# The second mixer of a two-block transformer on one core: from nineteen blocks between its projections to one block, head by head

## The reference, cut to what matters

```
u_a, v_a, q, k, v = jnp.split(h @ w_in, SPLIT_POINTS, axis=-1)
y_a = gelu(u_a) * (einsum('gtp,bcpgk->bctgk', tril(ws), rms_norm(gelu(v_a))) + bs)
q, k = rms_norm(q, q_norm_g), rms_norm(k, k_norm_g)          # per head of 128
z = einsum('bhqd,bhkd->bhqk', q, k) * 128 ** -0.5
log_fail = where(causal, log_sigmoid(-z), 0)                 # causal: key before query
log_a = log_sigmoid(z) + (sum of log_fail over the keys between key and query)
y_b = einsum('bhqk,bhkd->bhqd', where(causal, exp(log_a), 0), v)
y = rms_norm(concatenate([y_a, y_b]), out_norm_g)            # per group of 128
x = x + gate1 * (y @ w_out)
```

## Time and profile before

| | |
|---|---|
| median of three executions | 2900.5 us |
| the profiled execution, its own time | 2898.79 us |
| its span in the profile | 2897.1 us |
| PE busy, share of the span | 2436.1 us, 84% |
| DVE busy | 1146.4 us, 40% |
| ACT busy | 810.4 us, 28% |
| mean granted TensorE clock | 0.898 |

### The profile page before, as it was taken

The page is one execution under the profiler, slowest core; times in us unless marked ns, Lnnn a source line. Parts: engine busy times, 40 slices in busy tenths (PEclk is TensorE's granted clock), DMA queues, the critical chain, the costliest instruction groups (busy, mean ns, idle before and its releaser), DMA issues. The chain is left out here.

```text
span 2897.1 us, 42631 instructions
## 1 busy us (share of the span) xinstructions
PE 2436.1 (84%) x18072; PEld 1898.3 (66%) x18072; DVE 1146.4 (40%) x1421; ACT 810.4 (28%) x995; POOL 10.7 (0%) x56
## 2 busy tenths in 40 slices
PE   5998778977888978699999999996947577888885
PEld 5995558944875875499999899984833443444442
DVE  3763345533552410254555555554442220111112
ACT  3442323312121320244343443434420110111110
POOL 0000000000000000000000000000000000000000
PEclk8997989988885999899999999997978676999997
DMA  4446642467114322155555545523510469999998
GB/s 177 194 195 269 246 188 117 174 256 317 60 60 174 157 105 116 59 191 187 189 189 189 189 175 203 189 103 140 211 77 0 190 239 415 422 427 427 427 425 350
DMA packets 61371, 610.14 MB, mean 211 GB/s; under 512 B 8850, under 2 KB 9234, under 8 KB 16146
## 3 DMA queue, kind: packets, MB, share of 16 engines
q1 hardware_dynamic: 50114, 572.03, 49.6%
q0 software_dynamic: 1872, 23.07, 2.0%
q10 hardware_dynamic: 9216, 12.60, 1.2%
HBM read 674.76 MB, written 14.68 MB: 238 GB/s over the span
## 5 line engine op out<-in xcount | busy, mean ns | idle before, releaser
L1883 DVE TENSOR_TENSOR ffn_w_lo<-ffn_raw,ffn_w_hi 128x2048 fp32r<-128x2048 f32 x128 | 293.1, 2291 | 234.3 <-ACT ffn_w_hi L1876 234.3
L1876 ACT ACTIVATE ffn_w_hi<-ffn_raw 128x2048 fp32r<-128x2048 f32 x128 | 244.9, 1914 | 360.4 <-PE psum L1915 355.5
L1913 PE MATMUL psum<-u_hi,ffn_w_hi 128*128 128x256 f32 x1024 | 291.0, 284 | 15.1 <-DVE ffn_w_lo L1883 14.0
L1914 PE MATMUL psum<-u_lo,ffn_w_hi 128*128 128x256 f32 x1024 | 290.7, 284 | 0.0
L1915 PE MATMUL psum<-u_hi,ffn_w_lo 128*128 128x256 f32 x1024 | 290.7, 284 | 0.0
L2607 PE MATMUL psum<-moe_raw,moe_x_t 128*32 128x512 f32 x1536 | 216.6, 695 | 80.8 <-DMA moe_raw<-in_moe 73.2
L1913 PEld LDWEIGHTS psum<-u_hi,ffn_w_hi 128*128 128x128 f32 x1024 | 197.6, 193 | 16.0 <-DVE ffn_w_lo L1883 14.2
L1913 PE MATMUL psum<-ffn_w_hi,ffn_hid_hi 128*128 128x512 f32 x512 | 199.4, 389 | 0.0
L1914 PE MATMUL psum<-ffn_w_lo,ffn_hid_hi 128*128 128x512 f32 x512 | 199.4, 389 | 0.0
L1915 PE MATMUL psum<-ffn_w_hi,ffn_hid_lo 128*128 128x512 f32 x512 | 199.2, 389 | 0.0
L1914 PEld LDWEIGHTS psum<-u_lo,ffn_w_hi 128*128 128x128 f32 x1024 | 197.6, 193 | 0.5
(11 more groups left out here) (539 smaller groups left out, 4401.5 us busy)
## 6 DMA issues: line engine op xcount, KB each, us to landing
ring<-in_stream SPq DMA_DIRECT2D x107, 2048.0 KB, 10.9
moe_raw<-in_moe SPq DMA_DIRECT2D x96, 2048.0 KB, 17.0
ffn_raw<-in_ffn SPq DMA_DIRECT2D x128, 1024.0 KB, 4.8
moe_raw<-in_moe POOLq DMA_DIRECT2D x48, 2048.0 KB
expert_rows<-moe_stage ACTq DMA_DIRECT2D x192, 64.0 KB, 8.4
x<-in_x SPq DMA_DIRECT2D x2, 1024.0 KB, 7.8
mem<-in_mem SPq DMA_DIRECT2D x2, 1024.0 KB, 14.7
out<-x SPq DMA_DIRECT2D x2, 1024.0 KB, 4.4
```

Of the source, the lines that this page charges most:

```text
L1876: act.activation(self.w_hi[:, number % self.HIGHS], self.raw[:, number % self.RAWS], ACT.Copy)\
L1883: dve.tensor_tensor(self.w_lo[:, number % self.LOWS], self.raw[:, number % self.RAWS], self.w_hi[:, number % self.HIGHS].bitcast(F32), ALU ...
L1913: pe.matmul(out, lhs[0], rhs[0], start=start, stop=False)
L1914: pe.matmul(out, lhs[0], rhs[1], start=False, stop=False)
```

## The change

The function gets `sem`, to make 26 semaphores. The squares and sums of the groups 1, 2 and 3 are taken within the input projection: DVE does those of group g - 1 between pieces 3 and 4 of group g. Root, reciprocal, scaling and the mask on `ws` follow within that block too, while PE still works on group 4. The squares live in `h_t`, which is free once the input is split. SP no longer waits for the small inputs; DVE does, before the mask.

All that lay between the two projections is one block. q and k norm weights are applied by ACT's copy after the transposes. Per head ACT computes Abs of the scores, Exp of the negative and Ln(1 + e); DVE adds max(z, 0), masks for PE's sums, and subtracts; PE sums over keys in banks 4 to 7; DVE subtracts, ACT takes Exp, DVE masks, PE multiplies with v. The copy of the scores to SBUF and the separate maximum and argument are gone. The gating unit is computed while ACT is at the first heads, and its half of the output norm uses Ln and Exp for the root. The attention half is squared by ACT out of PSUM and scaled by DVE out of PSUM. The output norm's weights are applied as DVE takes the last transposes.

```diff
-def second_mixer(nc, k, io, x, h_t, gate, scope_sb):
+def second_mixer(nc, k, io, x, h_t, gate, scope_sb, sem):
...
+    spare = h_t[:].rearrange("p c t -> p (c t)")
+    squares = spare[:, 0:3 * TT * COLS].rearrange("p (t n) -> p t n", t=TT)
+    proj_summed, proj_root = sem("proj_summed"), sem("proj_root")
...
-            sp.wait_ge(k.small_in, 96)
...
+            def sums(g):
+                own, at = slice((g - 1) * COLS, g * COLS), proj[:, :, g * COLS:(g + 1) * COLS]
+                dve.wait_ge(k.tt_free, 4 + t0 + 2 * g + 2)
+                s.step(dve.tensor_tensor(squares[:, :, own], at, at, ALU.mult))
+                s.settle()
+                dve.tensor_reduce(ssq[:, :, 4 * g - 4:4 * g], squares[:, :, own].rearrange("p t (g n) -> p t g n", n=P),
+                                  AX.X, ALU.add).then_inc(proj_summed, 1)
+
+            def scaled(g):
+                at = proj[:, :, g * COLS:(g + 1) * COLS].rearrange("p t (g n) -> p t g n", n=P)
+                s.step(dve.tensor_tensor(at, at, ssq[:, :, 4 * g - 4:4 * g].unsqueeze(3).broadcast_to([P, TT, 4, P]),
+                                         ALU.mult))
+            s.step(dve.tensor_scalar(qk_norm[:, 0:1], col(k, "q_norm"), P ** -0.5, None, ALU.mult))
+            s.step(dve.tensor_copy(qk_norm[:, 1:2], col(k, "k_norm")))
             for g in range(5):
-                rows.low(dve, g, range(8))
+                rows.low(dve, g, range(4))
+                if g >= 2:
+                    sums(g - 1)
+                rows.low(dve, g, range(4, 8))
+            dve.wait_ge(proj_root, 1)
+            s.step(dve.reciprocal(ssq[:], ssq[:]))
+            s.settle()
+            for g in (2, 3, 1):
+                scaled(g)
+            dve.wait_ge(k.small_in, 96)
+            s.step(dve.tensor_tensor(ws[:], ws[:], const(k, "tri_le").unsqueeze(1).broadcast_to([P, GMLP_GROUPS, P]),
+                                     ALU.mult))
+            s.settle()
 
         @block.scalar
         def _(act):
@@ -2109,173 +2139,184 @@
                 if g:
                     take(g - 1)
                 rows.high(act, g, range(4, 8))
+            act.wait_ge(proj_summed, 3)
+            act.activation(ssq[:], ssq[:], ACT.Sqrt, bias=k.eps[:, 0:1], scale=1.0 / P).then_inc(proj_root, 1)
             take(4)
...
+    qk_t = spare[:, 0:2048].rearrange("p (a h n) -> p a h n", a=2, h=SB_HEADS)
+    y_sq = spare[:, 2048:4096].rearrange("p (a t g n) -> p a t g n", a=2, t=TT, n=P)
+    y, y_ssq = scope_sb("y", [P, TT, MIX_GROUPS, P]), scope_sb("y_ssq", [P, TT, MIX_GROUPS])
+    z, sp_, e = (scope_sb(n, [P, SB_HEADS, TT, T]) for n in ("sb_z", "sb_softplus", "sb_exp"))
+    y_t = sp_[:].rearrange("p h b q -> p (h b q)").rearrange("p (g t) -> p g t", t=T)
+    before, out_norm = const(k, "before"), cols_of(k, "out_norm")
...
+
+    def head(a, h):
+        return a[:, h].rearrange("p b q -> p (b q)")
+    with nc.Block(no_gpsimd_drain=True) as block:
+        @block.tensor
+        def _(pe):
+            def cumulate(h):
+                pe.wait_ge(passed, h + 1)
+                if h == 2:
+                    pe.wait_ge(gated_taken, 2)
+                ps = bank(k, 4 + h)
+                pe.matmul(ps[:, 0:T], const(k, "tri_gt"), e[:, h, 0, :], start=True, stop=False)
+                pe.matmul(ps[:, 0:T], const(k, "ones"), e[:, h, 1, :], start=False, stop=True)
+                pe.matmul(ps[:, T:2 * T], const(k, "tri_gt"), e[:, h, 1, :], start=True, stop=True).then_inc(summed, 1)
+
+            def attend(h):
+                pe.wait_ge(masked, h + 1)
+                if h == 0:
+                    pe.wait_ge(taken, 2)
+                for t in range(TT):
+                    for b in range(t + 1):
+                        mm = pe.matmul(bank(k, t)[:, h * P:(h + 1) * P], z[:, h, b, t * P:(t + 1) * P],
+                                       proj[:, b, 4 * COLS + h * P:4 * COLS + (h + 1) * P], start=(b == 0), stop=(b == t))
+                    if h == SB_HEADS - 1:
+                        mm.then_inc(attended, 1)
+            for a in range(2):
+                for t in range(TT):
+                    for h in range(SB_HEADS):
+                        at = (2 + a) * COLS + h * P
+                        mm = pe.transpose(bank(k, 2 * a + t)[:, h * P:(h + 1) * P], proj[:, t, at:at + P], const(k, "ident"))
+                    mm.then_inc(qk_turned, 1)
+            for t in range(TT):
+                for g in range(GMLP_GROUPS):
+                    mm = pe.matmul(bank(k, 6 + t)[:, g * P:(g + 1) * P], ws[:, g, :],
+                                   proj[:, t, COLS + g * P:COLS + (g + 1) * P], start=True, stop=True)
+                mm.then_inc(gated_mm, 1)
+            pe.wait_ge(qk_copied, 4)
+            for h in range(SB_HEADS):
+                for b in range(TT):
+                    mm = pe.matmul(bank(k, h)[:, b * T:(b + 1) * T], qk_t[:, 1, h, b * P:(b + 1) * P], qk_t[:, 0, h, :],
+                                   start=True, stop=True)
+                mm.then_inc(scored, 1)
+            for h in range(3):
+                cumulate(h)
+            attend(0)
+            cumulate(3)
+            for h in range(1, SB_HEADS):
+                attend(h)
+            pe.wait_ge(gated_scaled, 1)
+            pe.wait_ge(taken, 4)
+            for t in range(TT):
+                for g in range(4):
+                    mm = pe.transpose(bank(k, 2 + t)[:, g * P:(g + 1) * P], y[:, t, g, :], const(k, "ident"))
+                mm.then_inc(y_turned, 1)
+            for t in range(TT):
+                pe.wait_ge(y_scaled, t + 1)
+                for g in range(4):
+                    mm = pe.transpose(bank(k, 6 + t)[:, g * P:(g + 1) * P], y[:, t, 4 + g, :], const(k, "ident"))
+                mm.then_inc(y_turned, 1)
+
+            for a in range(2):
+                for t in range(TT):
+                    act.wait_ge(qk_turned, 2 * a + t + 1)
+                    act.activation(qk_t[:, a, :, t * P:(t + 1) * P], bank(k, 2 * a + t).rearrange("p (h n) -> p h n", n=P),
+                                   ACT.Copy, scale=qk_norm[:, a:a + 1]).then_inc(qk_copied, 1)
+            for h in range(SB_HEADS + 1):
+                if h < SB_HEADS:
+                    act.wait_ge(scored, h + 1)
+                    act.activation(head(e, h), bank(k, h), ACT.Abs).then_inc(sizes, 1)
+                if h:
+                    act.wait_ge(sizes, h)
+                    act.activation(head(e, h - 1), head(e, h - 1), ACT.Exp, scale=-1.0).then_inc(exp_done, 1)
+            for h in range(SB_HEADS):
+                act.wait_ge(exp_done, h + 1)
+                act.activation(head(e, h), head(e, h), ACT.Ln, bias=k.one[:, 0:1]).then_inc(ln_done, 1)
+            act.wait_ge(gated_summed, 1)
+            act.activation(y_ssq[:, :, 0:4], y_ssq[:, :, 0:4], ACT.Ln, bias=k.eps[:, 0:1], scale=1.0 / P)\
+               .then_inc(gated_ln, 1)
+            act.wait_ge(gated_ln, 1)
+            act.activation(y_ssq[:, :, 0:4], y_ssq[:, :, 0:4], ACT.Exp, scale=-0.5).then_inc(gated_root, 1)
+            for h in range(SB_HEADS):
+                act.wait_ge(logs, h + 1)
+                act.activation(head(z, h), head(z, h), ACT.Exp).then_inc(probs, 1)
+            for t in range(TT):
+                act.wait_ge(attended, t + 1)
+                act.activation(y_sq[:, 1, t], bank(k, t).rearrange("p (g n) -> p g n", n=P), ACT.Square).then_inc(squared, 1)
+            act.wait_ge(y_summed, TT)
+            act.activation(y_ssq[:, :, 4:8], y_ssq[:, :, 4:8], ACT.Sqrt, bias=k.eps[:, 0:1], scale=1.0 / P)\
+               .then_inc(y_root, 1)
+
+
+            def softplus(h):
+                dve.wait_ge(ln_done, h + 1)
+                s.step(dve.scalar_tensor_tensor(head(sp_, h), bank(k, h), 0.0, head(e, h), ALU.max, ALU.add))
+                s.settle()
+                dve.tensor_tensor(head(e, h), head(sp_, h), before, ALU.mult).then_inc(passed, 1)
+                dve.tensor_tensor(head(z, h), bank(k, h), head(sp_, h), ALU.subtract).then_inc(taken, 1)
+
+            def logs_of(h):
+                dve.wait_ge(summed, h + 1)
+                dve.wait_ge(taken, h + 1)
+                dve.tensor_tensor(head(z, h), head(z, h), bank(k, 4 + h), ALU.subtract).then_inc(logs, 1)
+
+            def mask(h):
+                dve.wait_ge(probs, h + 1)
+                dve.tensor_tensor(head(z, h), head(z, h), before, ALU.mult).then_inc(masked, 1)
+
+            def turned(n, src, part):
+                dve.wait_ge(y_turned, n + 1)
+                t, own = n % 2, slice(4 * part, 4 * part + 4)
+                s.step(dve.tensor_tensor(y_t[:, own, t * P:(t + 1) * P], src.rearrange("p (g n) -> p g n", n=P),
+                                         out_norm[:, own].unsqueeze(2).broadcast_to([P, 4, P]), ALU.mult))
+            for t in range(TT):
+                dve.wait_ge(gated_mm, t + 1)
+                dve.tensor_tensor(y[:, t, 0:4, :].rearrange("p g n -> p (g n)"), bank(k, 6 + t), gm_norm[:], ALU.mult)\
```

(86 more changed lines are left out.)

77 lines of the change are left out of this document (12 added, 65 removed).

## The result

The changed kernel took 2850.7 us (median of 2842.57, 2849.13, 2852.28 and 2854.14) against 2900.69 us before (2894.75 to 2901.26), a ratio of 0.983 with a 95% interval of 0.980 to 0.985. Run again beside other kernels it had a median of 2843.4 us against 2895.7 (ratio 0.983, 0.980 to 0.985).

The account below looks back on a forecast made before the run. Between the projections lie 87.7 us where no engine is the bound, a chain of blocks with barriers. 2898.8 - 46.8 = 2852.0 us for the profiled execution, 2853.7 from the median; forecast 2853, range 2844 to 2862.

Parts of the forecast that it names:

- Step 1: Norms' squares, sums, root, scaling and mask move into the input projection, hidden under TensorE: 14.5 us leave the path.
- the cover: Input projection: time to spare before TensorE wants piece 4 of a group, 4.8 us; without it 7.5 us are added.
- Step 2: The one block between the projections: output projection starts 40.2 us after block start, 46.8 us earlier including Step 1.
- stall of 1.7 us: In the block, DVE waits before logs(3) for TensorE's last sums over keys at the low clock: 1.7 us.
- The bound I gave for the high clock throughout: Between the projections: with TensorE at the high clock all through, the gain would be 49.8 us instead of 46.8.
- The first burst: Block's opening transposes, gating products and scores, taken at the high clock because TensorE was dense until 1.4 us before.
- Rival B: Low clock in the block's opening transposes, gating products and scores: first Ln at 18.6 instead of 13.3, 2858 us; chance 0.08.
- C: Abs and Exp in the block need different tables: 4 more table loads, 5.1 us, 2858 us; chance 0.06.
- D: Dear handoffs between engines on the block's path: 6 us more, 2859 us; chance 0.10.
- E: TensorE at the high clock throughout the block: 3 us less, 2850 us; chance 0.10.
- F: The input projection's slack is wrong: 7.5 us more, 2860.5 us; chance 0.03.
- G: TensorE loses its rest, output projection's 54.4 us run at the low clock: 2908 us at 100%; chance 0.03.

Follow-up runs that it names:

- e1: The kernel before, with only the norms' sums, root, scaling and mask moved into the input projection: 2885.8 us, ratio 0.996; gap between the projections 74.10 us.
- e3: The changed kernel with each group's squares and sum done twice in the input projection: projection 111.55 us, gap between the projections 37.10 us.
- e4: The changed kernel with each group's squares and sum done four times in the input projection: projection 123.60 us, gap between the projections 38.54 us.
- e7: The changed kernel with products nobody reads in TensorE's idle stretches: 2847.5 us, ratio 0.983; gap between the projections 36.24 us.
- e2: The changed kernel with squares, mask, sums, root and scaling back in three blocks behind the input projection: 2865.4 us, ratio 0.989; gap 53.21 us.
- e6: The changed kernel with the first transpose held back for two DVE passes, 4.7 us: gap between the projections 43.61 us.
- e10: The changed kernel with ten more blocks, each with one DVE copy of one column, ahead of its one block: gap between the projections 46.23 us.
- e5: The changed kernel with every step from Abs to the product with v waiting for all four heads: 2862.0 us, ratio 0.988; gap 52.08 us.
- e8: The changed kernel without the never-used quarter of each head, 384 instead of 512 columns: median 2841.6 us, ratio 0.982; gap 32.45 us.
- e9: The kernel of e8 with the gating half of the output projection's first two tiles inside the block: median 2834.7 us, ratio 0.979; gap 34.82 us.
- e0: The changed kernel run again unaltered: median 2843.4 us, ratio 0.983; gap between the projections 37.10 us.

## Why the prediction was right, and where a step of it failed

**What bounds it.** Right. The stretch was a chain, and 51.25 us of it went one for one.

**Step 1.** 14.5 us were worked out, 14.25 measured alone; that they agree so well is partly luck, since the clock gave 1.5 us and took 1.8 (e1). Cost to the projection nothing, as said (e3 shows even double work hidden). What I had for the cover, 4.8 us, is right to 0.2: with 7.4 us more each stall cost 2.8. The price without cover, 2.5 us a group, has the stall alone; in e4 the clock added 1.7 us behind two of the three stalls and nothing behind the third.

**Step 2 is where the sum was 4.4 us short,** and the step that failed is the clock in the second half, with instruction prices a little too high beside it. From the block's start, worked out and then measured: first softplus 13.3 and 12.6; masks done 30.1 and 26.9; last take done 39.6 and 35.1; output projection 40.2 and 35.8. Of the 4.4 us, 0.7 lie before the first softplus: the gating products start 1.8 us after the transposes and not 2.0, and ScalarE's instructions follow each other after about 0.5 us and not 0.60. 2.5 us lie between softplus and masks. There I held TensorE at the low clock for the sums of all heads, which gave the stall of 1.7 us before logs(3). In the trace it is low for the first head and most of the second only, and sums over keys of the last head start at once (2132.05). The stall did not occur. The other 0.8 is DVE's overlap of independent instructions, priced at 0.7 where 0.6 is nearer, less a wait for the first sums that was 0.49 us (2126.86) and not 0.15. The tail has the last 1.2 us: the gating half's transposes took 0.52 us for four and not 0.91. e4 is the counter-test that came unasked, with these cold and 1.4 us more.

The clock thus makes about 2.6 of the 4.4 us (the stall of 1.7 and the transposes), by this bookkeeping and not by a run of its own. The bound I gave for the high clock throughout, 49.8, was passed by the measured 51.25 although the clock was low in places; with the clock high throughout e7's gap would make it 52.1.

**The first burst** was at the high clock, as assumed, and e2, e6 and e10 show what the assumption was worth: 1.6 to 1.9 us. Rival B has its mechanism right and its price three times too high, against the very row that I quoted. The rule of the Trainium skill (TensorE: Matmul & The Clock Gate, "PE-mode transpose") that transposes don't count as activity did not hold in e6 either, where the gating products ran high right behind cold transposes.

**Table loads.** Exp's and Ln's loads took 1.28 us with the next instruction at once (2121.68 after 2120.38), no drain; Abs brought none, so C is out, and this agrees with "Table sets" in the Trainium skill's ScalarE: Activation LUTs. The load for the last Sqrt ran ahead of its wait (2138.48, its ACTIVATE at 2140.84), and the one for Exp after Ln (2124.44) was done before the first head's exponential could start (2127.58).

**The rivals.** D (dear handoffs) is refuted: the gap is shorter than with my price for them, and from the end of DVE's product with "before" (2123.15 plus 0.69) to TensorE's start (2123.90) pass 0.06 us. My price for cheap handoffs doesn't add up: 30 of them at 0.05 us instead of 0.2 are 4.5 us, not 3. E (high clock throughout) would be a gap of 36.24 (e7), 0.9 us below the measured one and 5.3 below the 41.5 worked out, where I had 3. F is refuted by the projection's 111.58 us and by e3. G is refuted: the output projection at 1.00 from 2149.4 on. What I held against G was misread, though: the input projection didn't stand right behind dense work, TensorE had been idle for 10.96 us before its first product at 2002.41.

**Sum.** 2898.8 - 51.25 is 2847.5; the medians stood 50.0 and 52.2 us apart in the two series. The forecast was 2 us off the first median and 10 off the second. The sum is 4.4 us short in both; the spread of the unchanged code takes 2 us off in the first series and adds 5 in the second. That the first median lies closer than the sum does is luck.

## What to carry to other kernels

Where a windows view shows the busy times of all engines adding up to the length of a stretch, the gain of merging its blocks can be summed instruction by instruction; here the sum gave 46.8 us of the 51.25. Of the 37.0 us of step 2, 15.0 are overlap of the heads (e5), about 8.6 barriers (e10) and 13.4 a remainder in which dropped passes, hidden work and the clock are not told apart. The worth of a part depends on what stands behind it: step 1 was worth 14.25 us before the old blocks and 16.1 before the new one, because the later bursts met another clock; why they did isn't shown. Price TensorE at both clock levels for every burst, and don't take the pessimistic level for all of them because the first is cold. In a stretch that one engine paces, cut that engine's columns (e8), and fill TensorE's idle time with real products of the next stage (e9), which earns their own time and the warm start.

## What the runs showed of the hardware

- A barrier between all engines costs 0.575 us where only DVE works in the blocks (e10).
- The granted clock stayed at 1.00 over 1.35 us of idleness, and TensorE was at the low level after 6.2 (e6). Three equal stalls of 2.65 us in one execution had three outcomes: low at once, low 0.9 us later, high throughout (e4).
- Sixteen transposes at the low level, with nothing else on TensorE, were followed by products at the high one in e6, and by products that were cold at first in e2 and e10 (2.41 and 2.45 us for 16 records against 1.95).
- The gap repeated to 0.01 us where nothing stalled ahead of it (the changed kernel, e0, e3), and was 1.4 us longer behind e4's stalls (38.54), in one execution with the same code and the same warm first burst. The clock of single bursts can thus move a block this short by 1.4 us.
- A DVE instruction of 512 columns that doesn't depend on the one before follows after 0.6 us though it takes 0.68 (2123.15, 2123.76, 2124.36 in the changed kernel).
